# Four stage seams: TensorE starts the next stage's first side unit before the barrier

## The reference

```
for l in range(DEPTH):                       # DEPTH = 2
    h = rmsnorm(x, norm_g[l])
    proj = jnp.einsum('bsd,de->bse', h, w_in[l])
    (a_q, a_k, a_v, a_z, b_q, b_k, b_v, b_z, c_qkv, c_z, c_b, c_a, gate_logits) = jnp.split(proj, offsets, axis=-1)
    o_a = windowed_gqa(...)                  # 8 heads, window 128
    o_b = diff_attention(...)                # 4 heads of two softmaxes each
    o_c = gated delta rule in chunks of 64, forward and backward, after a short convolution
    merged = sum over the three branches of sigmoid(gates) * (o * silu(z)) @ w_bo
    x = x + merged @ w_out[l]
return rmsnorm(x, final_g)
```

## Time and profile before

| | us |
|---|---|
| median of 3 runs (2817.09 to 2822.33) | 2818.3 |
| the profiled execution's own time | 2820.04 |
| span of the profiled execution | 2818.1 |
| PE busy, matmul | 2681.0 (95%) |
| DVE / ACT / POOL busy | 1473.8 / 1142.1 / 1242.4 |
| mean granted TensorE clock, share of full | 0.984 |

### The profile page before, as it was taken

The page is one execution under the profiler, slowest core; times in us unless marked ns, Lnnn a source line. Parts: engine busy times, 40 slices in busy tenths (PEclk is TensorE's granted clock), DMA queues, the critical chain, the costliest instruction groups (busy, mean ns, idle before and its releaser), DMA issues. The chain is left out here.

```text
span 2818.1 us, 39096 instructions
## 1 busy us (share of the span) xinstructions
PE 2681.0 (95%) x15158; PEld 2139.3 (76%) x15158; DVE 1473.8 (52%) x1835; ACT 1142.1 (41%) x1894; POOL 1242.4 (44%) x1128
## 2 busy tenths in 40 slices
PE   8989999999999999999999999899999999999998
PEld 4867767777778789778757677677777887897787
DVE  5136527776467343476240555377764764335742
ACT  3124425666365414341120344266663653244211
POOL 2464335443365450265434643444433654303753
PEclk9999999999999999999999999999999999999999
DMA  6253224232355545754243532333224664567442
GB/s 210 92 150 98 90 81 123 90 98 68 123 183 186 188 151 156 239 178 132 82 153 97 147 101 75 119 100 98 83 68 135 194 197 161 161 162 266 146 122 105
DMA packets 394072, 380.89 MB, mean 135 GB/s; under 512 B 90144, under 2 KB 332448, under 8 KB 393888
## 3 DMA queue, kind: packets, MB, share of 16 engines
q1 hardware_dynamic: 354912, 296.39, 34.8%
q10 hardware_dynamic: 38976, 82.00, 7.8%
HBM read 248.22 MB, written 130.09 MB: 134 GB/s over the span
## 5 line engine op out<-in xcount | busy, mean ns | idle before, releaser
L266 PE MATMUL pair<-h_hi,w_hi 128*128 128x512 f32 x1792 | 739.1, 412 | 74.1 <-PEq L203 39.2
L266 PE MATMUL pair<-h_hi,w_lo 128*128 128x512 f32 x1792 | 707.8, 395 | 0.0
L266 PE MATMUL pair<-h_lo,w_hi 128*128 128x512 f32 x1792 | 707.7, 395 | 0.0
L246 POOL TENSOR_TENSOR w_hi<-w_stage,masks 128x256 fp32r<-128x256 f32 x312 | 258.2, 859 | 640.9 <-PE pair L266 605.2
L266 PEld LDWEIGHTS pair<-h_hi,w_hi 128*128 128x128 f32 x1792 | 341.8, 191 | 196.1 <-issue 82.7
L266 PEld LDWEIGHTS pair<-h_hi,w_lo 128*128 128x128 f32 x1792 | 341.7, 191 | 75.5
L266 PEld LDWEIGHTS pair<-h_lo,w_hi 128*128 128x128 f32 x1792 | 342.7, 191 | 70.1 <-issue 5.3
L281 ACT ACTIVATE ev<-pair 128x512 f32<-128x512 f32 x224 | 132.9, 593 | 456.5 <-PE pair L266 455.6
L251 POOL TENSOR_TENSOR w_lo<-w_stage,w_hi 128x256 fp32r<-128x256 f32 x312 | 249.5, 831 | 6.1
L1691 POOL TENSOR_TENSOR w_lo<-w_stage,w_hi 128x256 fp32r<-128x256 f32 x128 | 149.9, 1201 | 169.0 <-ACT w_hi L1805 169.0
L1446 ACT ACTIVATE diff_p<-pair,diff_stat 128x1024 f32<-128x1024 f32 x128 | 143.1, 1118 | 126.1 <-DVE diff_stat L1549 122.2
(11 more groups left out here) (287 smaller groups left out, 4882.0 us busy)
## 6 DMA issues: line engine op xcount, KB each, us to landing
w_stage<-in_w_in SPq DMA_DIRECT2D x132, 512.0 KB, 4.1
proj<-ev ACTq DMA_DIRECT2D x132, 512.0 KB, 2.7
gate<-proj SPq DMA_DIRECT2D x48, 512.0 KB, 3.7
prep_x<-proj SPq DMA_DIRECT2D x24, 512.0 KB, 4.2
resid<-xT SPq DMA_DIRECT2D x16, 512.0 KB, 5.8
diff_vx<-proj SPq DMA_DIRECT2D x16, 512.0 KB, 3.3
prep_g<-gc_rows SPq DMA_DIRECT2D x16, 512.0 KB, 5.3
qd_t<-prep_eg SPq DMA_DIRECT2D x16, 512.0 KB, 2.6
```

The lines of the kernel that those rows point to most:

```text
L246: last = nc.gpsimd.tensor_tensor(w_hi[s][:, part], w_stage[s][:, part], bcast(ones, PIECE), ALU.mult)
L266: last = nc.tensor.matmul(bank(self.banks[half]), a[s][:, c, :], b[:, c, w], start=(c == 0 and n == 0), stop=(c == KC - 1 and n == 2))
```

## The change

- At four seams per layer (proj to win, win to diff, diff to prep, prep to delta) PE does the first half of the next stage's side unit 0 (`lead`, 24 matmuls) ahead of the barrier, behind its last work in the stage. It goes to bank 6, 0, 6 and 6. Its signal (side_sum) is set in advance, and ACT copies it first thing in the next stage.
- In win and diff the boundaries move so that each stage has as many halves between its barriers as before, the lead counted: win 5 ahead (numbers 0 to 4, 0 being the lead) and 2 behind, diff 4 and 4. In prep the first head takes halves 1 to 4 ahead of its first sum of squares, in delta 1 to 9 ahead of the first blocks.
- In win and diff the halves of the prologue go to banks 7 and 5 in turn, so that one need not wait for the copy of the one before. ACT copies the extra half (`side_out(4)` in win) ahead of its steps.

The diff, cut:

```
         SIDE = ["side_in0", "side_in1", "side_hi", "side_lo", "side_sum", "side_out", "side_put0", "side_put1"]
-        SIDE_AHEAD = {"side_in0": 16, "side_in1": 16, "side_hi": 2, "side_lo": 2}
-        SIDE_AHEAD_IN = {"side_in0": 16, "side_in1": 16, "side_hi": 1, "side_lo": 1}
+        SIDE_AHEAD = {"side_in0": 16, "side_in1": 16, "side_hi": 2, "side_lo": 2, "side_sum": 1}
+        SIDE_AHEAD_IN = {"side_in0": 16, "side_in1": 16, "side_hi": 1, "side_lo": 1, "side_sum": 1}
         SIGNALS, AHEAD = {}, {}
...
-            def __init__(self, l, q, per, banks=(7, 7)):
-                self.q, self.per, self.banks = q, per, banks
+            def __init__(self, l, q, per, banks=(7, 7), early=()):
+                self.q, self.per = q, per
+                self.bank_of = lambda n: early[n] if n < len(early) else banks[n % 2]
...
                     pe.wait_ge(q["side_lo"], START + turn * self.per + (k + 1))
                 if c == 0:
-                    late = 0 if self.banks[0] == self.banks[1] else 1
-                    pe.wait_ge(q["side_out"], START + turn * (2 * self.per) + max(2 * k + half - late, 0))
+                    n = 2 * k + half
+                    late = 0 if self.bank_of(n) == self.bank_of(n - 1) else 1
+                    pe.wait_ge(q["side_out"], START + turn * (2 * self.per) + max(n - late, 0))
                 w = slice(half * HALF, (half + 1) * HALF)
                 for n, (a, b) in enumerate(((w_hi, h_hi), (w_hi, h_lo), (w_lo, h_hi))):
-                    last = nc.tensor.matmul(bank(self.banks[half]), a[s][:, c, :], b[:, c, w], start=(c == 0 and n == 0),
+                    last = nc.tensor.matmul(bank(self.bank_of(2 * k + half)), a[s][:, c, :], b[:, c, w], start=(c == 0 and n == 0),
                                             stop=(c == KC - 1 and n == 2))
                 if c == KC - 1:
...
                     act.wait_ge(q[f"side_put{s}"], START + turn * (16 * self.in_slot[s]) + 16 * (k // 2))
                 act.wait_ge(q["side_sum"], START + turn * (2 * self.per) + (2 * k + half + 1))
-                nc.scalar.activation(ev[s][:, half * HALF:(half + 1) * HALF], bank(self.banks[half]), ACT.Tanh if gate else ACT.Copy,
+                nc.scalar.activation(ev[s][:, half * HALF:(half + 1) * HALF], bank(self.bank_of(2 * k + half)), ACT.Tanh if gate else ACT.Copy,
                                      scale=0.5 if gate else scale).then_inc(q["side_out"], 1)
...
+        def lead(pe, into):
+
+            for c in range(KC):
+                for n, (a, b) in enumerate(((w_hi, h_hi), (w_hi, h_lo), (w_lo, h_hi))):
+                    nc.tensor.matmul(bank(into), a[0][:, c, :], b[:, c, 0:HALF], start=(c == 0 and n == 0),
+                                     stop=(c == KC - 1 and n == 2))
+
+        LEAD_WINDOW, LEAD_FULL, LEAD_GATES = 6, 0, 6
         g_next = small[:, 32:32 + KC]
         g_row = w_stage[0][:].rearrange("p k e -> p (k e)")
...
                         .then_inc(q["gc_turned"], 1)
                     with pe.Fori(4, pairs_of_units) as i:
                         units(i)
+                    pe.wait_ge(q["w_lo0"], START + pairs_of_units + 1)
+                    lead(pe, LEAD_WINDOW)
                 @block.scalar
...
                       for r in range(4)]
                 xr_of = lambda r: XR[min(r, 3)]
                 UNITS = 16
-                side = Side(l, q, UNITS)
+                side = Side(l, q, UNITS, early=(LEAD_WINDOW, 7, 5, 7, 5))
                 side_unit = lambda k: U_BQ + k if k < UNITS else diff_unit(0, k - UNITS)
                 side_column = lambda k: side_unit(k) * P + (N_BA if k == UNITS else 0)
-                FIRST, LAST = 4, 3
+                FIRST, LAST = 5, 2
                 shared = (6, 10, 14, 18, 22, 26, 30)
                 side_steps = [n for n in range(STEPS) if n not in shared]
...
                     turn_values()
                     side_half(2)
                     side_half(3)
+                    side_half(4)
                     for n in range(STEPS):
                         scores(n)
...
                     turn(STEPS - 1)
                     side_half(tail_half(1))
                     sum_values(QUADS - 1)
-                    side_half(tail_half(2))
+                    pe.wait_ge(q["side_lo"], START + UNITS + 1)
+                    lead(pe, LEAD_FULL)
                 @block.scalar
...
                     side_out(3)
+                    side_out(4)
                     for n in range(STEPS):
                         o = (3 - window(n)[2]) * P
...
                     side_out(tail_half(1))
-                    side_out(tail_half(2))
                     side.finish(act, 1)
...
                 XR0 = (XR, ZT)
                 UNITS = 4 * HEADS
-                side = Side(l, q, UNITS)
+                side = Side(l, q, UNITS, early=(LEAD_FULL, 7, 5, 7))
                 side_unit = lambda k: diff_unit(k // 4, k % 4)
                 side_column = lambda k: side_unit(k) * P + (N_BA if k % 4 == 0 else 0)
                 is_gate = lambda k: k % 4 == 0
-                FIRST, LAST = 3, 5
+                FIRST, LAST = 4, 4
                 QUARTERS = [(n, slot) for n in range(STEPS) for slot in ((0, 1) if n % 2 == 0 else (0,))]
                 assert FIRST + len(QUARTERS) // 2 + LAST == 2 * UNITS
...
                                                     start=True, stop=True)
                         last.then_inc(q["total"], 1)
-                    for n in range(FIRST):
+                    for n in range(1, FIRST):
                         side_half(n)
                     for n in range(STEPS):
...
                     side_half(tail_half(3))
-                    side_half(tail_half(4))
+                    pe.wait_ge(q["side_lo"], START + UNITS + 1)
+                    lead(pe, LEAD_GATES)
                 @block.scalar
...
                             act.wait_ge(q["gated"], START + h)
                         nc.scalar.activation(ZT[:], VX[:], ACT.Tanh, scale=0.5).then_inc(q["tanh"], 1)
+                    side_out(0)
                     for n in range(2):
-                        side_out(n)
+                        side_out(n + 1)
                         high(0, n)
-                    side_out(2)
+                    side_out(3)
                     act.wait_ge(q["lsum"], START + 2)
                     nc.scalar.activation(lexp, lsum, ACT.Exp).then_inc(q["lexp"], 1)
...
                     side_out(tail_half(3))
-                    side_out(tail_half(4))
                     side.finish(act, 1)
...
                     for h in range(4):
                         half = lambda n: side.half(pe, 0, 4 * h + n // 2, n % 2)
-                        half(0)
-                        half(1)
-                        if h == 0:
-                            half(2)
-                            half(3)
+                        if h:
+                            half(0)
+                            half(1)
+                        else:
+                            for n in range(1, 5):
+                                half(n)
                         total(h, 1)
-                        half(2 if h else 4)
+                        half(2 if h else 5)
                         total(h, 0)
-                        half(3 if h else 5)
-                        half(4 if h else 6)
+                        half(3 if h else 6)
+                        if h:
+                            half(4)
                         products(h)
                         pe.wait_ge(q["log"], START + 2 * h + 2)
...
                             half(6)
                         half(7)
+                    pe.wait_ge(q["side_lo"], START + PREPARED + 1)
+                    pe.wait_ge(q["side_out"], START + 2 * PREPARED - 1)
+                    lead(pe, LEAD_GATES)
                 @block.scalar
...
+                            out_half(0, 4)
                         else:
                             out_half(h, 0)
...
                         to_exp(1, h)
-                        out_half(h, 2 if h else 4)
+                        if h:
+                            out_half(h, 2)
                         out_half(h, 3 if h else 5)
                         tanh(2, h)
...
                                                             start=True, stop=True)
                         last.then_inc(q["levels"], 1)
-                    for n in range(EARLY):
+                    for n in range(1, EARLY):
                         side_half(n)
                     for stage in range(4):
...
                                                             ACT.Copy, scale=-1.0)
                         last.then_inc(q["moved"], 1)
+                    side_out(0)
                     act.wait_ge(q["w_raw_in"], START + 16)
                     nc.scalar.activation(W[:, 0], RAW0.rearrange("p r c -> p c r"), ACT.Copy).then_inc(q["w_copied"], 1)
                     act.wait_ge(q["w_in"], START + 16)
```

(2 more changed lines are left out.)

57 lines of the change are left out of this document (34 added, 23 removed).

## The result

| | before | changed |
|---|---|---|
| median, us (runs) | 2819.02 (4) | 2842.03 (4) |
| lowest to highest | 2817.09 to 2822.33 | 2840.07 to 2844.78 |
| profiled execution, own time and span | 2820.04, 2818.1 | 2840.07, 2838.2 |
| mean granted clock | 0.984 | 0.982 |

The change is **slower by 0.79%** (ratio 1.0079, 95% interval 1.0066 to 1.0091), some 23 us. The forecast was 2824 with a range up to 2830. PE's busy time is the same in both profiles (2681.0 and 2680.9 us), so the longer span is time in which PE stands still: 137.1 us before, 157.3 now.

A forecast was written before the change was run, and what follows sets the result against it. PE's idle time at four seams per layer (39.2 us over 8 barriers) was what the change could close, mostly lost again at prologue gates: -5.3 without the clock, +11 for it, 2825.7 profiled, about 2824 median; range 2808 to 2830.

The forecast's parts named there:

- The direction: Whole kernel: slower than before by more than the 0.2% edge, chance 0.37.
- Step 1, proj to win: Seam proj to win: PE's 5.4 us idle goes, other engines start 0.5 later; +0.5 / +0.5 us by layer.
- Step 2, win: Win: the gain is lost in the prologue waiting for POOL's w_lo of unit 2; +0.6 / +0.6 us.
- Steps 3 and 4, diff: Diff: waits for k_lo and w_lo, +0.9 / -0.8 us; seam to prep closes, -4.2 / -4.4 us.
- Step 5, prep: Prep: ACT's chain to k_tok sets the time, seam to delta closes; 0 / +1.4 us without clock.
- Step 6, delta: Delta: half 2 waits 7.7 us for w_lo of unit 1, then eight halves to the blocks; -0.4 / 0 us.
- The clock: New long waits in win, diff, prep and delta lower PE's clock: 5.5 us per layer, +11 in all.
- the waits chain: Rival: ACT and DVE lack slack after win's or prep's prologue, so 5.5 us is lost per layer; 2835, chance 0.08.
- The prologues give way: Rival: gates are softer than read, most seam time is gained; 2765 in full, nearer 2800, chance 0.14.
- three signs of being wrong: Win shorter by over 1 us, its unit 2 w_lo before 33 us behind the barrier, or PE idle down over 20.
- the waits for w_lo that I expected by stage: PE's waits for POOL's w_lo rise from 6.2 to some 40 us: win 12, diff 2, prep 1, delta 8 per layer.

The follow-up runs named there:

- e1_sines: Changed kernel with POOL in win splitting units 6 and 7 ahead of sines (4) and (5); 2831.0 us, ratio 1.0040.
- e2: Changed kernel without the repeated split of unit 1 at the start of win; 2841.2 us, ratio 1.0076.
- e3: Changed kernel with unit 1 of delta split at the end of prep instead of behind the barrier; 2835.7 us, ratio 1.0061.
- e5_before_nosplit1: Kernel before the change, without the repeated split of unit 1 at the start of win; 2820.9 us, ratio 1.0008.
- e10_gates_prep: e9_gates plus, in prep, ACT copying half 1 and making w_hi of unit 2 ahead of its first tanh; 2791.9 us, ratio 0.9905.
- e9_gates: Changed kernel with e1_sines, e2, e3 edits, earlier unit 2 weights (win, diff), win's prologue reordered, an eleventh half before delta's blocks; 2802.8 us, ratio 0.9938.
- e8: Kernel before the change with only the diff-to-prep lead, and prep's first head as in the change; 2828.4 us, ratio 1.0027.

## Why the prediction was wrong

The direction had a chance of 0.37 and came; the size did not: 14 us are missing against the profiled execution, 18 against the median.

1. *Step 1, proj to win: right within the scatter.* +0.5 / +0.5 forecast, +0.7 / -0.5 measured. The seam idles 0.3 at the barrier.
2. *Step 2, win: wrong, the largest error.* The gate in the prologue was right: w_lo of unit 2 at 186.3 is 32.9 behind the barrier (33.5 before), and the stage was to be as long as before but for 1.2. The step that failed is one that the sum put at nothing: I looked at the prologue alone and took the main part as unchanged, because the number of halves is. But every half moved by one step against the sines and their loads, and a wait of 2.6 with 1.6 of low clock behind it (the half from 269.06 lasted 7.35 in place of 5.75) came up. e1_sines shows it: 4.6 and 3.9 of the 5.0 and 4.0 us. That term is worth 8 to 11 us in all. In the prologue I had missed the wait for V: PE's 13.1 us there (6.7 for V, 6.4 for w_lo) are 7.4 more than before, near the 8 forecast, since the moment of w_lo alone fixes their sum.
3. *Steps 3 and 4, diff: right in kind, mis-sized.* Waits for k_lo (2.9 and 3.5) and w_lo came where they were forecast. Over the four kernels with this code of diff (the change, e1, e2, e3) its length was 337.9, 338.0, 339.8, 340.0, 340.3, 340.3, 340.6 and 341.2, mean 339.7. With the old code it was 340.0 and 340.5 before, and 340.8 and 341.4 in e5_before_nosplit1, mean 340.7: -1 rather than -2.6 and -4.5. Two terms failed. The clock I put at +0.7: in the second layer scores and half 4 took 2.28 and 7.70 in place of 1.66 and 5.75, 2.6 in all. And of the -4.2 of the seam some 2.5 was given back in the steps by new waits: PE waits 1.0 for a copy of ACT at 572.32 and 644.87, where there was none, and 0.1 longer at each of five more. No experiment separates the two terms; they are read from the trace.
4. *Step 5, prep: right* (+2.1 / +3.5). PE's turn behind k_tok starts 48.5 behind the barrier, 48.65 forecast. That all of it hung on ACT's order, and could in part be had back, only e10_gates_prep showed.
5. *Step 6, delta: right but for one link.* PE waits 7.65 for w_lo of unit 1, which ends 13.4 to 13.5 behind the barrier as before. The eight halves to 1043.85 take 46.5, 2.5 more than 8 x 5.5, where 2.1 of clock was forecast. The forecast stopped there. The blocks then wait 1.0 and 1.3 for DMAs that ACT issues behind half 8's copy:

```profile
1038.51 0.60 ACT L283 ACTIVATE ev<-pair 128x512 f32<-128x512 f32 x1 [4.90 <-PE pair L268]
1038.59 0.83 ACTq L1980 DMA_DIRECT2D delta_t<-solved  x2
1039.45 1.90 ACTq L1983 DMA_DIRECT2D delta_u<-solved  x4
```

   PE's blocks start at 1044.88, 6.4 behind that copy's start, while half 9 takes 5.5. In the earlier trace rows it had just come in time; I had read that start as set by PE.
6. *The clock: right in kind, but I had read a rule out of the rows that does not hold.* +11 forecast. By the prediction, waits of 3.3 us or more lower the clock and one of 2.07 does not. In the changed kernel one of 2.60 at 266.46 lowered it, and one of 2.86 at 442.21 did not. Already the trace of before has one of 2.04 with the low clock behind it:

```profile
1574.56:1576.60 2.04, 0.00 (x0) 1.00 0.53 217
1576.60:1582.34 5.74, 5.74 (x18) 0.70 0.37 106
```

   And in e9_gates PE stood still for 3.85, from 795.91 to 799.76, and the clock stayed high behind it:

```profile
799.76:806.50 6.74, 6.74 (x34) 1.00 0.13 39
```

   So in these traces the length of a wait does not tell whether the clock falls. PE's unchanged busy time says what the new waits cost in clock: about as much as the old seams had, which the forecast put at 8 x 2.2 = 18, while it gave the new waits 11. The Trainium skill's price (TensorE: Matmul & The Clock Gate, "HAM oscillation — how this bites in real kernels") is half of the time spent at the low clock. By it, as an estimate, the stretch of 6.94 at a mean of 0.70 lost 0.30 x 6.94 = 2.1, and that of 8.22 at 0.66 lost 2.8; the rows say 1.95 (7.70 in place of 5.75) and 2.5. The trace agrees within 0.3, and no half here was slow throughout.

Of the rivals, "the waits chain" (2835) was nearest in time, but not in mechanism: softmax and roots had slack (PE waits 0.2 us in all from 194 to 262, and the view shows no wait from 784 to 806), and what chained was POOL's queue. "The prologues give way" is refuted by the stage lengths of the changed kernel, and for the seam of diff to prep by e8 alone. Of the three signs of being wrong that I had named, two did not come (win was longer, and PE's idle time rose by 20 instead of falling); the third, w_lo of unit 2 earlier than 33 us behind the barrier, was met by 0.1. The waits for w_lo that I expected by stage add up to 46, not to the "some 40" of the text; 40.9 came (36.8 + 4.1), since in win 6.7 of the 12 fell on V.

## What to carry to other kernels

Closing a seam was worth nothing here, since the stage behind it started at gates of its own. List, for each prologue, which row ends last, remove it, and read again, since the next one stands right behind (7.65 became 5.7 in delta; DMA behind POOL, then ACT behind POOL in win). When a count of halves is shifted against the steps, compare every queue that mixes both kinds of work through the whole stage, not the prologue alone. An edit can be good only together with another: with leads the new order of win's prologue won 9 us per layer (e9_gates against e1_sines), without them orders that are related, but not the same, lost 4 to 10, and leads alone lost 12 per layer; together, with delta and prep, they give -1%.

## What the hardware showed beyond that

In the changed kernel POOL's w_hi of a unit, four pieces of 128x256, took 2.79 us at 157.72 and 5.73 at 177.74: a piece takes about 0.73 or about 1.7 us. In the second place the three slow pieces lie beside DVE's work with two SBUF operands (L1071, L1076, L1080), and the fast one overlaps it by 0.1 us only. Over the whole trace, 95 of the 768 pieces take more than 1.3 us, and all 95 overlap work of DVE. The Trainium skill (SBUF — State Buffer, "Who interferes with whom") tells of a port pair that DVE and GpSimd share under an exclusive lock. The trace fits, but no run here separates it from other causes. The forecast had taken the durations of before at the same places, so it cost nothing there, but any move of a split to another place should be priced at both ends.

The same code of diff came out at 337.9 to 341.2 in eight stretches. The two shortest are those in which the clock stayed high behind the wait for k_lo (2.86 us in one, 3.13 in e1_sines).
